# Two column groups in turn, an earlier feed-forward start, reordered splits: one change to a float32 encoder layer

## The reference, cut to what matters

```python
h = _layernorm(ALPHA * h + mix, ln1_g[l], ln1_b[l])
ff = (jax.nn.silu(h @ w_ffn_gate[l]) * (h @ w_ffn_up[l])) @ w_ffn_down[l]
h = _layernorm(ALPHA * h + ff, ln2_g[l], ln2_b[l])
```

## Time and profile before

| | us |
|---|---|
| median of 3 runs | 1760.29 |
| lowest, highest | 1758.29, 1761.35 |
| the profiled execution: its own time | 1762.14 |
| its span from first to last instruction | 1760.4 |
| PE busy in it | 1726.2 |
| DVE, ACT busy | 1187.2, 832.2 |
| mean granted TensorE clock | 0.995 of full |

### The profile page before, as it was taken

The page is one execution under the profiler, slowest core; times in us unless marked ns, Lnnn a source line. Parts: engine busy times, 40 slices in busy tenths (PEclk is TensorE's granted clock), DMA queues, the critical chain, the costliest instruction groups (busy, mean ns, idle before and its releaser), DMA issues.

```text
span 1760.4 us, 19539 instructions
## 1 busy us (share of the span) xinstructions
PE 1726.2 (98%) x8292; PEld 1447.6 (82%) x8292; DVE 1187.2 (67%) x997; ACT 832.2 (47%) x680; POOL 94.5 (5%) x87
## 2 busy tenths in 40 slices
PE   9999999999999999999999998999999999799999
PEld 8888888998888888888888876878787878678887
DVE  5765656677766745445666769797979797664445
ACT  5454544454544445444454525455455546453332
POOL 0000002222211300000000000000000000000000
PEclk9999999999999999999999999999999999899999
DMA  9667655454444557656888758787878785985553
GB/s 347 246 238 225 201 191 192 161 174 177 163 166 166 182 186 260 225 178 249 263 279 285 296 186 256 231 245 228 252 219 247 243 241 161 273 254 194 195 196 131
DMA packets 121329, 387.36 MB, mean 220 GB/s; under 512 B 8608, under 2 KB 43808, under 8 KB 102688
## 3 DMA queue, kind: packets, MB, share of 16 engines
q1 hardware_dynamic: 112384, 364.56, 61.4%
q0 software_dynamic: 2720, 10.49, 3.3%
q10 hardware_dynamic: 6144, 11.14, 1.7%
HBM read 359.82 MB, written 25.69 MB: 219 GB/s over the span
## 4 chain that ended last, share of the span: by engine, by line
PE 84%; DVE 9%; DMA 3%; issue 2%; ACT 1%; SPq 1%; DVEq 0%
PE pair L1963 16%; PE pair L1965 16%; PE pair L1964 16%; PE pair L1937 9%; PE pair L1935 5%; PE pair L2235 3%; PE pair L2234 3%; PE pair L2233 3%; DVE part_lo L1694 2%; PE side L2042 2%; PE side L2213 2%; PE side L2215 2%; PE side L2214 2%; DMA ff_land<-ff_scratch 1%; DMA raw<-in_stream 1%
## 5 line engine op out<-in xcount | busy, mean ns | idle before, releaser
L1255 DVE TENSOR_TENSOR weight_lo<-raw,weight_hi 128x2048 fp32r<-128x2048 f32 x213 | 489.0, 2298 | 377.9 <-ACT weight_hi L870 376.6
L870 ACT ACTIVATE weight_hi<-raw 128x2048 fp32r<-128x2048 f32 x213 | 408.1, 1916 | 539.0 <-DMA raw<-in_stream 538.6
L1963 PE MATMUL pair<-weight_hi,act_both 128*128 128x512 f32 x672 | 267.8, 399 | 3.9 <-DVE weight_lo L1255 3.9
L1965 PE MATMUL pair<-weight_hi,act_both 128*128 128x512 f32 x672 | 261.9, 390 | 0.0
L1964 PE MATMUL pair<-weight_lo,act_both 128*128 128x512 f32 x672 | 261.7, 389 | 0.0
L1937 PE MATMUL pair<-act_both,weight_hi 128*128 128x512 f32 x600 | 211.3, 394 | 0.0
L1154 ACT ACTIVATE part_hi<-part_raw 128x2048 fp32r<-128x2048 f32 x60 | 114.2, 1912 | 158.3 <-DMA part_raw<-in_stream 49.5
L1935 PE MATMUL pair<-act_both,weight_lo 128*128 128x256 f32 x640 | 172.8, 280 | 0.0
L1694 DVE TENSOR_TENSOR part_lo<-part_raw,part_hi 128x2048 fp32r<-128x2048 f32 x60 | 136.5, 2281 | 34.4 <-ACT part_hi L1154 34.4
L1963 PEld LDWEIGHTS pair<-weight_hi,act_both 128*128 128x128 f32 x672 | 126.2, 188 | 30.8 <-DVE weight_lo L1255 4.4
L1963 PE MATMUL pair<-weight_hi,ff_both 128*128 128x512 f32 x352 | 138.6, 394 | 12.7 <-DVE ff_both L1679 12.7
(11 more groups left out here) (304 smaller groups left out, 2792.6 us busy)
## 6 DMA issues: line engine op xcount, KB each, us to landing
raw<-in_stream SPq DMA_DIRECT2D x259, 1024.0 KB, 5.2
part_raw<-in_stream SPq DMA_DIRECT2D x30, 1024.0 KB, 6.7
scratch<-spill ACTq DMA_DIRECT2D x40, 256.0 KB, 4.3
part_raw<-in_stream POOLq DMA_DIRECT2D x10, 1024.0 KB, 10.8
ln_rows<-in_ln_rows SPq DMA_DIRECT2D x6, 1024.0 KB, 11.3
gate<-scratch SPq DMA_DIRECT2D x12, 512.0 KB, 6.6
ff_scratch<-ff_blocks SPq DMA_DIRECT2D x11, 512.0 KB, 6.0
ff_land<-ff_scratch SPq DMA_DIRECT2D x44, 128.0 KB, 8.3
```

The costliest lines, as they stand in the source:

```text
L870: act.activation(hi_of(n), raw_of(n), ACT.Copy).then_inc(extra_h if extra(n) else h_ready, 1)
L1255: dve.tensor_tensor(lo_of(n), raw_of(n), hi_of(n).bitcast(F32), ALU.subtract)\
L1963: pe.matmul(out, hi[:, k0 + k, tok], w_hi[:, k, :], start=first and k == 0, stop=False)
L1965: mm = pe.matmul(out, lo[:, k0 + k, tok], w_hi[:, k, :], start=False, stop=last and k == 3)
```

## The change

It has three parts.

1. Down phase: pieces are taken in the order (0,0), (1,0), (0,1), (1,1), ... for c=0 and c=1, then c=2 and c=3 as before. A newly fetched group is needed at every second piece. Ring slots are shifted by one so that D2 can be loaded before D3. `round_ff` and `lo_of_ff` stand at every second piece, and the loads of `z` and of the norm's rows move to D18 to D21.
2. Start: the first tile of `z` is stored before F4 is loaded, the second after F4 is used; plain piece 0 is loaded first of the plain ones; `act_sum` is made in halves (`act_total`), the first inside the norm of the second tile; F5's `split_lo` comes before two of the forms; the gate product moves ahead of the blocks.
3. Blocks: `part_split(p, 2)` and `plain_split(p, 1)` come before `sum_t4` and `gate_others`; both `turn_ff` come later, and their `save_ff` on SP too.

```diff
+DOWN_ORDER = [(m % 2, m // 2) for m in range(22)] + [(2 + m // 11, m % 11) for m in range(22)]
...
         def plain_slot(m):
-            return (m + 2) % 3
+            return m % 3
...
             load_part(0, 0, W_E)
+            sp.wait_ge(h_done, 12)
+            sp.dma_start(h_scratch[0:P, :], z[:, 0, :]).then_inc(z_out, 16)
             loads(first + 4, first + 6)
             sp.wait_ge(h_done, 16)
             load_part(0, 0, W_A)
             loads(first + 6, first + 8)
-            for t in range(TT):
-                sp.dma_start(h_scratch[t * P:(t + 1) * P, :], z[:, t, :]).then_inc(z_out, 16)
             sp.wait_ge(piece_used, first + 5)
+            load_plain(0, 0)
+            sp.dma_start(h_scratch[P:T, :], z[:, 1, :]).then_inc(z_out, 16)
+            sp.wait_ge(piece_used, first + 6)
             load_plain(0, 1)
...
+            for c in range(5, 11):
+                load_down(2 * c - 4)
+                load_down(2 * c - 3)
+                fetch_ff(c)
             sp.wait_ge(z_out, 32)
             for t in range(TT):
+                load_down(18 + t)
                 sp.dma_start(z[:, t, :], h_scratch[t * P:(t + 1) * P, :]).then_inc(z_back, 16)
...
+            def act_total(t):
+                tok = slice(t * P, (t + 1) * P)
+                dve.wait_ge(piece_used, FIRST["ffn"])
+                dve.wait_ge(turned_l, 12 + 4 * t)
+                dve.tensor_tensor(act_sum[:, :, tok], act_hi[:, :, tok].bitcast(F32), act_lo[:, :, tok].bitcast(F32),
+                                  ALU.add).then_inc(act_summed, 1)
...
-                if m in (13, 24, 35):
-                    c = (m - 2) // 11 - 1
+                if m in (22, 24, 35):
+                    c = {22: 0, 24: 1, 35: 2}[m]
...
-                if m < FF_COLUMNS:
-                    pe.wait_ge(ff_l, m + 1)
+                if c == 0:
+                    pe.wait_ge(ff_l, q + 1)
```

More of the change, by code:

```diff
@@ L701, in load_down @@
                     sp.wait_ge(piece_used, n.c - 3)
-                sp.dma_start(raw_of(n), stream[FIRST["down"] + m]).then_inc(landed(n)[0], 16)
+                c, q = DOWN_ORDER[m]
+                sp.dma_start(raw_of(n), stream[FIRST["down"] + FF_COLUMNS * c + q]).then_inc(landed(n)[0], 16)
             def save_ff(c):
@@ L743, in _ @@
                 load_part(p, 1, W_A)
-                save_ff(2 * p - 1 if p else 0)
                 load_plain(p, 3)
@@ L747, in _ @@
                 load_part(p, 1, W_B)
-                if p:
-                    save_ff(2 * p)
                 load_plain(p, 4)
@@ L752, in _ @@
                 load_part(p, 1, W_E)
+                if p:
+                    save_ff(2 * p - 1)
                 load_plain(p, 5)
                 load_plain(p, 6)
+                save_ff(2 * p)
                 if p == BLOCKS - 1:
@@ L784, in _ @@
             sp.wait_ge(plain_used, PLAIN * BLOCKS)
-            load_down(2)
+            load_down(3)
             save_ff(9)
             fetch_ff(3)
+            load_down(4)
+            save_ff(10)
+            load_down(5)
+            sp.wait_ge(ff_turned, 11)
+            fetch_ff(4)
+            for c in range(5, 11):
+                load_down(2 * c - 4)
+                load_down(2 * c - 3)
+                fetch_ff(c)
             sp.wait_ge(z_out, 32)
             for t in range(TT):
+                load_down(18 + t)
                 sp.dma_start(z[:, t, :], h_scratch[t * P:(t + 1) * P, :]).then_inc(z_back, 16)
-            save_ff(10)
-            load_down(4)
-            sp.wait_ge(ff_turned, 11)
-            fetch_ff(4)
-            load_down(5)
-            fetch_ff(5)
-            for m in range(6, 11):
-                load_down(m)
-                fetch_ff(m)
             for r in range(2):
+                load_down(20 + r)
                 gain_and_bias(ln2_rows, 4, r, rows2_in)
-                load_down(11 + r)
-            for m in range(13, 44):
+            for m in range(22, 44):
                 load_down(m)
@@ L1776, in _ @@
             a21, a22 = act_sum[:, 0:8, P:T], act_sum[:, 8:16, P:T]
+            act_total(1)
             split_lo(Nth(n + 4))
-            dve.wait_ge(turned_l, 16)
-            dve.tensor_tensor(act_sum[:], act_hi.bitcast(F32), act_lo.bitcast(F32), ALU.add).then_inc(act_summed, 1)
-            split_lo(Nth(n + 5))
-            dve.wait_ge(act_summed, 1)
+            dve.wait_ge(act_summed, 2)
             dve.tensor_tensor(form_raw[:, F_A5], a21, a22, ALU.subtract).then_inc(form_made, 1)
@@ L1804, in _ @@
                 plain_split(p, 0)
-                if p:
-                    turn_ff(2 * p - 1)
-                else:
-                    dve.wait_ge(piece_used, n + 8)
-                    wait_taken(dve, g)
-                    dve.tensor_tensor(silu[:, 1], plain_pair()[:], silu[:, 1], ALU.mult).then_inc(pair_free[(g + 1) % 2], 1)
-                    wait_taken(dve, g + 1)
-                    turn_ff(0)
+                part_split(p, 2)
+                plain_split(p, 1)
+                if not p:
                     lo_of_form(F_N4)
@@ L1833, in _ @@
                 part_split(p, 8)
+                if not p:
+                    wait_taken(dve, g + 1)
+                turn_ff(2 * p)
                 part_split(p, 9)
@@ L1848, in _ @@
             split_lo(Nth(DOWN + 1))
-            lo_of_ff(1)
             turn_ff(9)
             gate_others(p)
-            lo_of_ff(2)
+            lo_of_ff(1)
             split_lo(Nth(DOWN + 2))
             turn_ff(10)
+            lo_of_ff(2)
             split_lo(Nth(DOWN + 3))
-            lo_of_ff(3)
             g0 = GROUP["down"]
@@ L1859, in _ @@
                 split_lo(Nth(DOWN + m))
-                if m < FF_COLUMNS:
-                    lo_of_ff(m)
-                if m in (13, 24, 35):
-                    c = (m - 2) // 11 - 1
+                if m < 20 and m % 2 == 0:
+                    lo_of_ff(m // 2 + 1)
+                if m in (22, 24, 35):
+                    c = {22: 0, 24: 1, 35: 2}[m]
                     dve.wait_ge(z_back, 32)
-                    dve.wait_ge(piece_used, DOWN + 11 * (c + 1))
+                    dve.wait_ge(piece_used, DOWN + (21, 22, 33)[c])
                     residual(g0 + c, c)
```

38 lines of the change are left out of this document (20 added, 18 removed).

## The result

| | before | changed |
|---|---|---|
| median of 4 runs each, us | 1760.82 | 1746.95 |
| lowest, highest | 1758.29, 1761.60 | 1743.19, 1748.85 |
| the profiled execution | 1762.14 | 1745.96 |
| its span | 1760.4 | 1744.3 |

The ratio is 0.9921, 95% interval 0.9901 to 0.9941: faster by 13.9 us. I had forecast 24.9 us, 1735.4, with 1742 as the upper end. The direction was right, the size was not, and the time lies outside the range.

The account below looks back on a forecast made before the run. TensorE was taken as the bound, busy 1726.2 of 1760.4 us. Gains of 15.3 (down phase), 6.1 (blocks) and 3.5 (start) summed to 24.9 us, giving 1735.4 us against the 1760.3 median; range 1731 to 1742, forecast's chance 0.62.

Parts of the forecast that it names:

- Down phase, 15.3 forecast: Down phase: the whole wait goes, 12.7 us plus 2.2 for the clock plus 0.1 for each other restart; lower bound 10.8.
- the long wait: Down phase: the 8.3 us wait at D4, with 2.2 us more lost to the half-speed clock behind it.
- the DMA engines set the pace there: Down phase before the change: splits of pieces with a fetch stand 6.63 us apart, leaving 4.2 us for a fetch.
- Rival D: Down phase: a piece needs 6.63 us with or without a fetch, 31.3 us of waiting, total 1766.7; chance 0.03.
- Start, 3.5 forecast: Start: F5 and F6 without waits, F7 after 5.3 us idle, P2 at 1087.8 against 1091.26; gain bounds 8.8 and -1.1.
- F0 to F4 have none: Start: PE has no wait at F0 to F4, so the first half of `act_sum` counts nothing.
- I take 8.4: Start: the second store of `z` takes 8.4 us, between bounds 4.8 and 12.9, and lands at 1062.5.
- rival A: Start: the store of `z` lands late, near 12.9 us; the start gives -1.1, time 1740.0; chance 0.12.
- Blocks, 6.1 forecast: Blocks 1 to 4: P2's waits go, 4 x (1.43 + 0.1) us; zero at the worst, no more at the best.
- The displaced work: Blocks: the DVE work moved behind P2's split ends at 1259.8, P3's split at 1262.0 against its turn at 1264.5.
- Rival E: Whole kernel: each removed wait comes back at the next place, nothing is left, time 1760; chance 0.03.
- B: Down phase: DMA still sets the pace by a pair taking 11.4 us, 4.5 us lost, time 1739.9; chance 0.12.

## Why the prediction was wrong

**Down phase, 15.3 forecast, 16.5 measured: right, the size a little low.** All waits on `ff_both` went, D22 does not wait for `residual`, and the clock is 1.00. The idle time was the 12.7 us I had counted. The missing 1.2 us is the clock: I gave 2.2 us to the long wait and 0.1 to each other restart, and PE's busy time in the stretch fell by 3.7 (243.22 to 239.50).

**But the reason for the pace was mis-stated.** I wrote that "the DMA engines set the pace there", with 4.2 us for a fetch, as if 6.63 us were the price of a piece with its fetch. With `z` late a piece with its fetch came every 5.2 us in the old order, so a fetch costs at most 5.2 - 2.46 = 2.7 us on this reading, and 5.8 - 2.46 = 3.3 in the run with D4's load moved. The 6.63 showed only in the backlog that follows the two megabytes of `z`. Rival D was priced from the same 6.63 and had even less ground than I gave it. The forecast survived since two pieces share a fetch and there is room for either figure, and the run with early `z` shows that room: the same two megabytes in the same place cost 1.7 us of the stretch, 1.08 of them a wait.

**Start, 3.5 forecast, 0.7 measured: the mechanism right, the term mis-sized.** F5 and F6 start without a wait, as worked out, plain 0 too; F7's start is tied to the store's landing (1065.15 + 7.2 = 1072.36, forecast 7.1). I had misread one place: "F0 to F4 have none" is wrong, F4 had waited 0.78 us for its split, a wait that the earlier trace rows do not show. It waits 0.84 now, so nothing of the sum hangs on it. The term that failed is "I take 8.4": the store took 10.07 us, and 10.3 and 10.4 in two other runs. That is 1.7 us. The other 1.1 us is the clock behind the gap: F7 was forecast at 5.5 + 1.7 = 7.2 us and took 8.26. That term is no firmer than this: in the five other executions with the same start, F7 took 7.00 to 8.32 us after a gap of 6.9 to 7.1. In the store's time my 8.4 was nearer to the 10.07 than rival A's 12.9; in the gain its -1.1 was nearer to the 0.7 than my 3.5. I had the two bounds from rows, 4.8 and 12.9, and chose between them by transfers that only read HBM, although the 10.6 of the earlier trace rows, the first of the two stores, was the nearest row: by it the store lands at 1064.7 and the gain is 3.5 - 2.2 = 1.3. The Trainium skill, "DMA: Bandwidth & Descriptors", section "Where the ~2 µs actually goes", warned that a write into HBM may have a long receipt. Its fit, given there for DMAs issued by GpSimd, would make a lone megabyte 4.4 us as an estimate; this store took 10.1 to 10.5 in ten executions, each time beside other loads, so it stays open how much of this is receipt and how much company.

**Blocks, 6.1 forecast, -0.1 measured: wrong, and this is most of the miss.** P2's waits did go, as worked out. The failed step is "The displaced work": I followed DVE up to P3 and SP's saves to the next block's part, and stopped. What is late next was not on DVE. Plain 4 needs ACT's `silu`, which stands behind P8's half, which stands behind the accumulating DMA. The margin there was 2.3 us. Without the wait at P2, PE comes 1.3 us sooner (1289.31 against 1290.64 in block 2), which alone would have left 1.0. But the DMA was issued 0.4 us later (1275.72 against 1275.33) and took 1.9 us longer: 2.3 - 1.3 - 0.4 - 1.9 = -1.3, the wait that PE shows. The 1.9 come from the gain itself: PE reaches the end of plain 2 1.5 us sooner, which releases plain 5's load onto that DMA, while DVE, which now transposes shortly before the sum that POOL waits for, lets the DMA go 0.4 us later. Two runs show both links: with the gate copy first the stretch is 397.13 with the DMA still slow, and with the load held back it is 397.12 with the copy still second. 404.2 - 397.1 = 7.1 us is the forecast's 6.1 and a little more (a removed wait gives back 0.3 us beyond its own length, where I had put 0.1): the gain was real, and one instruction's place away. I had written that the save "now waits in front of the load of the next block's first part" and priced that at nothing, without asking which loads go *earlier* because PE does.

**The total.** 1.2 - 2.8 - 6.2 on the three parts, -1.0 before F4 and -0.1 in the tail make -8.9 of the 24.9 us, which leaves the 16.0 of the spans; the medians say 13.9, since the profiled execution of before lay 1.3 us above its median and that of the changed kernel 1.0 below. Rival E, nothing gained because each wait comes back at the next place, was right for the blocks and for them alone. I had given it 0.03 for the whole. Priced for each part by itself it would have put 1735.4 + 6.1 = 1741.5 beside A and B, and together with the store's 1.7 us 1743.2, past my upper end. Two of my sums are off by 0.1 and change nothing: five restarts besides the long wait make 15.4 and not 15.3, and the upper bound of the store's time gives -1.0 and not -1.1.

## What to carry over

When a wait on the critical engine is removed, list every instruction of that engine up to the next wait of the *same period*, with its releaser and how early that releaser is, and take the smallest margin as the bound on the gain; a margin on another engine's queue (here 2.3 us, behind a DMA that then took 1.9 longer) counts like any other. A copy that only frees PSUM belongs ahead of work that waits for a DMA. And when the critical engine gets ahead, ask which transfers its progress releases sooner, not only which ones the new order makes later: they can land on top of the one that matters.

## What the runs showed of the hardware

- A DMA store of 1 MB to HBM took 10.1 to 10.5 us from issue to landing in ten executions, with loads in flight beside it, and 12.7 to 13.0 in the four where it was issued right behind another store; a lone 1 MB load took 4.8.
- An accumulating DMA from POOL and a plain load from SP, 1 MB each, traded landing times with their order of issue: 10.1 and 10.1 us with POOL 1.9 us ahead, 12.0 and 7.1 us when issued together (block 2, before and changed).
- Four fetch parts of 128 KB landed after a median of 6.6 us right behind a 1 MB load and 3.7 us behind a 512 KB save.
- The same traffic of a piece and a fetch was served every 5.2, 5.8 or 6.6 us in three executions of the old group order. In the slowest, two megabytes of `z` had gone ahead. What sets the difference was not settled.
- The clock's fall after a gap of 6.85 us cost 2.65 us (clock 0.65 over 8.4), after one of 3.57 us 2.5 (clock 0.50 over five). For the same piece after gaps of 6.9 to 7.1 us the cost ranged from 1.6 to 2.9 over six executions, against its 5.44 us at full clock.
